# A mixture-of-experts layer whose expert weights are loaded as one contiguous 16 KB piece per partition

## The reference

```
def hier_moe(h, w_grp, b_grp, w_exp, b_exp, w_gate_e, w_up_e, w_down_e):
    ...                                   # one group of 4 per token, 2 experts of the 4 in it: combine (288, 16)
    a = jnp.einsum('td,edf->tef', t, w_gate_e)          # 16 experts, (2048, 512) each
    u = jnp.einsum('td,edf->tef', t, w_up_e)            # (2048, 512)
    hid = jax.nn.silu(a) * u * combine[..., None]
    return jnp.einsum('tef,efd->td', hid, w_down_e)     # (512, 2048)
```

## Time and profile before

| | |
|---|---|
| median of 3 runs | 2122.38 us |
| the profiled execution, its own time | 2116.29 us |
| its span | 2114.7 us |
| PE busy | 1763.7 us (83%) |
| DVE, ACT, POOL busy | 435.5, 242.9, 199.8 us |
| mean granted TensorE clock | 0.923 of full |
| read from HBM | 524.10 MB |
| queue q1 (SP): packets, MB | 180324, 439.58 |
| queue q0 (POOL): packets, MB | 21888, 111.73 |
| expert weight loads | 96 of 2048 KB, median 22 us from issue to landing |

### The profile page before, as it was taken

The page is one execution under the profiler, slowest core; times in us unless marked ns, Lnnn a source line. Parts: engine busy times, 40 slices in busy tenths (PEclk is TensorE's granted clock), DMA queues, the critical chain, the costliest instruction groups (busy, mean ns, idle before and its releaser), DMA issues.

```text
span 2114.7 us, 24773 instructions
## 1 busy us (share of the span) xinstructions
PE 1763.7 (83%) x9405; PEld 1116.8 (53%) x9405; DVE 435.5 (21%) x855; ACT 242.9 (11%) x421; POOL 199.8 (9%) x363
## 2 busy tenths in 40 slices
PE   6589999999989999995877899998686777777771
PEld 3156666666667777774555677777322222222220
DVE  2010000000065633322444211103111010101015
ACT  2010000000011101112333200002301010101011
POOL 1011110201010001401111000000100000000000
PEclk9899999999999999997999999997888988898885
DMA  9988586777344335428999854241499999999993
GB/s 366 416 327 316 186 297 221 286 263 248 114 131 136 124 114 171 136 99 303 356 365 364 330 208 154 84 159 80 144 387 377 387 382 387 380 383 379 385 363 144
DMA packets 210553, 552.43 MB, mean 261 GB/s; under 512 B 19221, under 2 KB 56267, under 8 KB 187099
## 3 DMA queue, kind: packets, MB, share of 16 engines
q1 hardware_dynamic: 180324, 439.58, 56.8%
q0 software_dynamic: 21888, 111.73, 15.4%
q10 hardware_dynamic: 8288, 0.39, 0.3%
HBM read 524.10 MB, written 27.57 MB: 261 GB/s over the span
## 4 chain that ended last, share of the span: by engine, by line
PE 61%; DMA 22%; SPq 6%; DVE 5%; issue 4%; DVEq 1%; ACT 1%; POOL 0%; POOLq 0%; ACTq 0%; PEldq 0%
PE ps L636 57%; DMA ring<-in_w_up_e_dram 9%; PE ps L646 4%; SPq L435 4%; DMA xT<-in_w_ada_dram 3%; DMA ring<-in_w_ada_dram 2%; DMA ring<-in_cache_v_dram 2%; DMA ring<-in_cache_k_dram 2%; DMA z<-h_rows,xT 1%; DMA y_rows<-z,xT 1%; SPq L377 1%; DVE ring L1358 1%; SPq L383 1%; DVE ring L1364 1%; DVE z L1367 0%
## 5 line engine op out<-in xcount | busy, mean ns | idle before, releaser
L636 PE MATMUL ps<-hT,ring 128*128 128x288 f32 x2560 | 650.0, 412 | 8.4 <-ACT hT L1181 6.5
L636 PEld LDWEIGHTS ps<-hT,ring 128*128 128x128 f32 x2560 | 484.1, 192 | 179.9 <-issue 52.1
L636 PE MATMUL ps<-ring,work 128*64 128x512 f32 (+1 forms) x1280 | 287.5, 661 | 94.8 <-DMA ring<-in_w_up_e_dram 67.0
L1367 DVE COPY z<-ps 128x256 f32<-128x256 f32 (+8 forms) x122 | 78.5, 648 | 958.0 <-PE ps L636 892.9
L636 PE MATMUL ps<-z,ring 128*128 128x288 f32 (+1 forms) x1040 | 256.0, 407 | 5.1 <-PE ps L636 3.4
L636 PEld LDWEIGHTS ps<-ring,work 128*64 128x64 f32 (+1 forms) x1280 | 94.3, 143 | 284.4 <-issue 244.0
L636 PE MATMUL ps<-ring,z 128*32 128x128 f32 (+3 forms) x1824 | 214.4, 453 | 30.5 <-DMA ring<-in_cache_v_dram 11.3
L636 PEld LDWEIGHTS ps<-z,ring 128*128 128x128 f32 x1040 | 196.5, 190 | 63.0 <-issue 7.6
L646 PE MATMUL ps<-ident,z 64*128 64x64 f32 (+4 forms) x644 | 79.4, 274 | 97.0 <-DMA z<-h_rows,xT 44.2
L636 PEld LDWEIGHTS ps<-ring,z 128*32 128x32 f32 (+2 forms) x1824 | 83.3, 130 | 132.6 <-issue 125.3
L646 PEld LDWEIGHTS ps<-ident,z 64*128 64x128 f32 (+4 forms) x644 | 63.8, 156 | 125.2 <-issue 114.1
(11 more groups left out here) (198 smaller groups left out, 814.6 us busy)
## 6 DMA issues: line engine op xcount, KB each, us to landing
ring<-in_w_in_dram SPq DMA_DIRECT2D x40, 2048.0 KB, 12.6
xT<-in_w_ada_dram POOLq DMA_DIRECT2D x64, 1024.0 KB, 7.1
ring<-in_w_gate_e_dram SPq DMA_DIRECT2D x32, 2048.0 KB, 22.5
ring<-in_w_up_e_dram SPq DMA_DIRECT2D x32, 2048.0 KB, 21.1
ring<-in_w_down_e_dram SPq DMA_DIRECT2D x32, 2048.0 KB, 22.9
ring<-in_w_ada_dram SPq DMA_DIRECT2D x16, 2048.0 KB, 25.1
ring<-in_cache_k_dram SPq DMA_DIRECT2D x64, 512.0 KB, 12.7
ring<-in_cache_v_dram SPq DMA_DIRECT2D x64, 512.0 KB, 9.3
```

The source lines that it names most:

```text
L636: return nc.tensor.matmul(o, lhsT, rhs, start=start, stop=stop, skip_group_check=free)
L1367: return nc.vector.tensor_copy(o, a)
```

## The change

The weights are assigned to the partitions in another way. Of gate and up, partition p now gets the 16 consecutive channels 16p to 16p+15, of down the 4 consecutive channels 4p to 4p+3. What one partition gets in one load is then one contiguous piece of 16 KB in HBM: before it was 8 pieces of 2 KB (gate, up) or 2 of 8 KB (down). Bytes, slots, number of loads and waits stay the same. So that the other side of the products agrees, the transposes take every 16th column of `hg` and every 4th of `hid`.

```diff
@@ -427,13 +427,10 @@
                     if n < 4:
-                        src = io[("w_gate_e", "w_up_e")[n % 2]][0, ds(e, 1), (n // 2) * 8 * P:(n // 2 + 1) * 8 * P, :]
-                        k = 8
+                        src = io[("w_gate_e", "w_up_e")[n % 2]][0, ds(e, 1)].rearrange("a (p k) n -> p (a k n)", p=P)[:, n // 2 * SLOT:(n // 2 + 1) * SLOT]
                     else:
-                        src = io["w_down_e"][0, ds(e, 1), (n - 4) * 2 * P:(n - 3) * 2 * P, :]
-                        k = 2
-                    sp.dma_start(slot(s).rearrange("p (k n) -> p k n", k=k),
-                                 src.rearrange("a (k p) n -> p (a k) n", p=P)).then_inc(sem(f"ring_full{s}"), 16)
+                        src = io["w_down_e"][0, ds(e, 1)].rearrange("a (p k) n -> p (a k n)", p=P)[:, (n - 4) * SLOT:(n - 3) * SLOT]
+                    sp.dma_start(slot(s), src).then_inc(sem(f"ring_full{s}"), 16)
@@ -1132,7 +1129,7 @@
                 for k in range(KT):
-                    last = tr(ps[:, 1 + k // 8, (k % 8) * W:(k % 8 + 1) * W], hg[:, k * P:(k + 1) * P])
+                    last = tr(ps[:, 1 + k // 8, (k % 8) * W:(k % 8 + 1) * W], hg.rearrange("t (p k) -> t k p", k=KT)[:, k, :])
@@ -1158,7 +1155,7 @@
                 for f in range(4):
-                    last = tr(ps[:, 3, f * W:(f + 1) * W], hid[:, f * P:(f + 1) * P])
+                    last = tr(ps[:, 3, f * W:(f + 1) * W], hid.rearrange("t (p f) -> t f p", f=4)[:, f, :])
```

## The result

| | before | changed |
|---|---|---|
| median | 2124.61 us (11 runs, 2119.51 to 2129.85) | 2137.71 us (11 runs, 2128.53 to 2148.69) |
| ratio, 95% interval | | 1.0065 [1.0044, 1.0086] |
| the profiled execution | 2116.29 us | 2148.69 us |
| loop: down products of window 0 to window 15 | 526.1 us | 546.3 us |
| packets on q1, the queue of the loads | 180324 | 118884 |

The change makes the kernel slower by 13 us. The forecast was 2115 us, faster by 7. The profiled execution of the changed kernel is the slowest of its 11 runs. Of the 32.4 us between the two profiled executions 20.3 lie in the expert loop; 10.1 us had passed before it begins, in code that is the same (POOL issues the gather at the head of the loop at 1514.18 us before and at 1524.29 after). So the profile says where the loss is, and the medians how large it is.

The account below looks back on a forecast made before the run. Weight loads bound the late windows (35.6 us), a ring of waits nearly as long being next. Windows of 35.0 against 35.07 us gave -1, the last window -5; taking -7, 2122.4 became 2115 us, range 2090 to 2156.

Parts of the forecast that it names:

- the circle: Expert loop: gather, transposes, down products, copy, scatter, next gather, which POOL issues only after the scatter landed; 34.14 us before.
- The bound of the loads: Expert loop, DMA time per window: weight loads plus 3.9 us beside them, predicted to go from 35.6 to 33.5 us.
- The transposes: PE, 16 + 4 per window: operand columns now 64 or 16 bytes apart, predicted to add 0.3 us per window.
- the sum of the circle: Expert loop window: 16.6 + 8.0 + 10.1 = 34.7 us, plus 0.3 for transposes, 35.0 against 35.07 before.
- The gather: Small transfer in the expert loop, meeting gate and up loads: predicted 10.1 us, from 8.67 before.
- rule of turns: DMA engines: q0 and q1 alternate one packet each; a scatter has 8 turns per engine, a gather 4.
- The scatter: Small transfer in the expert loop: predicted 8.0 us, sharing two or three turns with the second down load, from 8.86.
- full contention: Rival, chance 0.15: all 8 turns of the scatter meet 16 KB packets; 38.3 us per window, 2162 us.
- dry spell: Queue q1 after the down products: second down load ends at 9.3 us, gate load flows from 10.0, letting scatter packets run free.
- Loads still bound it: Rival, chance 0.20: scatter stays 7.0 us and gather 8.7, so the loads' 33.5 us decide the window; 2098 us.
- Strided transposes cost double: Rival, chance 0.17: spread operand columns add 2.4 us a window; 2147 us.
- Cut again: Rival, chance 0.08: the queue cuts load pieces into 2 or 4 KB packets, so only the order changes; 2122 us.

Follow-up runs that it names:

- the loads alone: Changed kernel with weights in 16 KB pieces but transposes taking adjacent columns as before, so results are not the reference's; 2134.04 us, ratio 1.0050 against the kernel before.

## Why the prediction was wrong

**The steps that held.** That the gain of the loads runs into a second bound, the circle, and that PE would wait for the gather: in every window. The packet: 228 packets, 3.41 MB, in a stretch of 8 us with q1 alone are 208 of 16 KB at 16 x 8 us / 208 = 615 ns (20 are small), 616 reckoned.

```profile
DMA packets 228, 3.41 MB, mean 426 GB/s; under 512 B 20, under 2 KB 20, under 8 KB 20
...
q1 hardware_dynamic: 228, 3.41, 100.0%
```

That is DMA from 1730 to 1738 us. The bound of the loads, 33.5: measured 33.48 once the circle was open. The transposes, 0.3 us: 2.50 us for 20 after a wait, where it was 2.38, both at a granted clock of 0.50, the lower of its two levels (1.2 GHz). The last window, 30: 29.9; no load meets the gather there, so the error below does not enter. That the loads would be 2.1 us cheaper a window also held, though its price of 5.43 us for 2 KB pieces came from the rate of 386 GB/s; 64 packets of 89 ns would have made 5.70, because the packets' times overlap (share 104.5%).

**The step that failed** is the sum of the circle, 35.0 us, against 36.9 measured; it was the comparison 35.0 against 35.07 that made "faster". Two terms of it were too small.

*The gather, taken at 10.1 us, took 11.2.* The term gave it four turns of a q1 packet each, and the price of a packet was that of q1 alone. DMA from 1722.7 to 1729.7 us, while the gather issued at 1717.84 ran:

```profile
DMA packets 152, 1.71 MB, mean 245 GB/s; under 512 B 22, under 2 KB 22, under 8 KB 22
...
q1 hardware_dynamic: 86, 1.29, 71.5%
q0 software_dynamic: 66, 0.42, 26.5%
```

1.29 MB are 79 packets of 16 KB, and 0.715 x 16 x 7 us / 79 = 1.01 us each, not 0.62. The engines are busy (0.98) but move 245 GB/s instead of 426. This is not peculiar to 16 KB. The gather's own packets are slow even when nothing runs beside them, as in the kernel before from 1514 to 1519 us:

```profile
q0 software_dynamic: 80, 0.52, 43.2%
```

0.432 x 16 x 5 us / 64 = 0.54 us for 8 KB, where a load's packet of that size takes 0.315. And in the kernel with 8 KB pieces, from 1707.3 to 1710.8 us, beside the gather issued at 1703.18:

```profile
q1 hardware_dynamic: 55, 0.45, 52.5%
q0 software_dynamic: 63, 0.52, 50.6%
```

0.525 x 16 x 3.5 us / 55 = 0.53 us for 8 KB instead of 0.315. With prices from stretches that have both parties in them, four turns cost 4 x (1.01 - 0.53) = 1.9 us more with 16 KB than with 8 KB; measured, 11.2 against 9.1. So the rule of turns held and its price did not.

The prediction's own bound, 2.1 us over 8.67, so 10.8, was no bound, since both of its prices, 616 and 89 ns, were of packets that ran alone. It also gave a gather one 2 KB packet per turn; from 1560.9 to 1563.9 us the trace before has 125 packets of q1 (0.26 MB) beside 56 pieces of the gather. From that bound I had then taken 1.3 because two gathers (8.67, 8.91) differed little, which says nothing of 16 KB.

*The scatter, taken at 8.0 us, took 8.2 in the mean of 12 windows and 11.1 to 12.3 in three* (from issue to landing). Those three have the length of the rival "full contention". DMA rows of a good window (1601.5 to 1604.5 us) and of a bad one (1636.5 to 1642.5):

```profile
q1 hardware_dynamic: 61, 0.74, 58.5%
q0 software_dynamic: 134, 0.48, 39.4%
```

```profile
q1 hardware_dynamic: 143, 2.08, 82.0%
q0 software_dynamic: 134, 0.49, 19.9%
```

The scatter's packets are the same number in both. In the good window 0.74 MB of q1, 45 packets of 16 KB, pass in 3 us, under three for each engine: the two or three turns of the forecast. The bad window starts like it (q1 has a share of only 8.4% from 1637.2 to 1638.2), but the gate load began when part of the scatter was still to go. Its last 3.5 us, 1639 to 1642.5:

```profile
q1 hardware_dynamic: 92, 1.49, 99.3%
q0 software_dynamic: 8, 0.02, 1.7%
```

0.02 MB are six of the 128 pieces. In the trace the last four of them start 0.76 us apart, which is one packet of 16 KB (0.615) and one of its own (0.16): one lagging engine holds up the landing of all. The window of 1780.92 ends in the same way; in that of 1558.44 half of the scatter was still to go after 7.5 us (0.27 MB of it pass from 1565.9 to 1569), with no such dry spell before, and there the contention was broad. My timeline treated the sixteen engines as one, and the dry spell in it was 0.7 us. On the mean of the 15 windows the scatter takes 9.5 us until POOL goes on, instead of 8.0 + 0.55: 0.95 more.

The gather's 1.1 and the scatter's 0.95 make 37.05 of the forecast's 35.0. What is neither gather nor scatter took 16.7 us on the mean, where I had 16.6 + 0.3, so 0.2 less: 36.9, as measured. Why some windows fall on one side is open, and so is why a gather's packets, and those beside them, are slow. Open is also why the changed kernel's runs spread over 20 us: the profile with the loads alone has three windows over 11 us as well, and took 2131.62 us where this one took 2148.69.

The measured 2137.7 lies in the range of 2090 to 2156, and 0.37 stood on slower. That is no merit of the sum: the likeliest case said faster, and the slower ones were priced at 2147 and 2162 for other reasons, or for more windows, than what came.

**The rivals.** "Loads still bound it" needed the circle at 32.3 and was wrong as long as POOL closes it. "Strided transposes cost double" was near on the engine at full clock (2.00 instead of 1.20 us for 16, 1.7 times) and wrong in price (the doubling was a bound of mine, from no row): on the circle, behind the wait for the gather, 20 of them take 2.50 instead of 2.38 us. "Cut again" was wrong: q1 has 61440 packets fewer, which is 64 x (1024 - 128) + 32 x (256 - 128), so every load went out in 128 pieces.

## What to carry to other kernels

A transfer that is made cheaper only counts until the next ring of waits, and a ring that holds small DMAs gets longer by the very packets that make the bulk loads efficient: choose the piece size of bulk loads by who shares the engines with them. When two bounds lie within 2% of one another, first open the latency ring (here by issuing the gather one step earlier), since then the piece size hardly matters here (the opening alone, with the loads of before, gained 0.2%); either remedy, early gather or 8 KB pieces, turns a loss of 0.65% into a gain of 0.9 to 1.1%. A sum that comes out within 0.1 us of the old window says "same" with errors on both sides, not "faster"; and the price of contention has to come from a stretch with both parties in it.

## What was unexpected in the hardware

While the indirect gather of 64 rows of 8 KB ran, the DMA engines were busy but moved 245 GB/s instead of 426, and 16 KB packets beside it took 1.01 us instead of 0.615, 8 KB packets 0.53 instead of 0.315. Even with nothing beside it, its 8 KB packets took 0.54 us. A transpose whose weight operand has its columns 64 bytes apart took 0.125 us instead of 0.075 (2.00 and 1.20 us for 16, granted clock 1.00), but 0.125 instead of 0.119 where PE came out of a wait (2.50 and 2.38 us for 20, granted clock 0.50).
